# Attention in the second block: the values become the stationary operand, the turned probabilities move

## The reference

```python
def step(args):                       # causal, for 128 queries
    logits = jnp.einsum('bhqd,bhkd->bhqk', qc, k)
    if log_decay is not None:         # the forgetting attention
        logits = logits + args[2][..., None] - log_decay[:, :, None, :]
    logits = jnp.where(key_idx[None, :] <= q_idx[:, None], logits, -jnp.inf)
    p = jax.nn.softmax(logits, axis=-1)
    return jnp.einsum('bhqk,bhkd->bhqd', p, v)
# memory heads
p = jax.nn.softmax(jnp.einsum('bshd,bmhd->bhsm', q, k), axis=-1)
o_mem = jnp.einsum('bhsm,bmhd->bshd', p, v_mem)
x = x + jnp.concatenate([o_mix, o_mem], axis=-1) @ w_out[i]
```

## Time and profile before

| | us |
|---|---|
| median of 3 runs | 1580.07 |
| lowest and highest | 1578.89, 1580.39 |
| the profiled execution, its span from the first to the last instruction | 1580.1 |
| PE busy / DVE busy / ACT busy / POOL busy in it | 1545.3 / 824.7 / 736.3 / 322.4 |
| forgetting attention, about | 490 to 576 of the span |
| latent attention, memory heads, about | 1036 to 1077 of the span |
| latent attention, its 12 heads, about | 1077 to 1161 of the span |

### The profile page before, as it was taken

How to read it: one execution, slowest core, us unless ns; L and a number is a source line. 1 busy time by engine, 2 the same in 40 slices (tenths; PEclk the granted TensorE clock), 3 DMA queues, 4 the chain that set the end, 5 groups by cost and what they waited for, 6 DMA issues and landing times. The chain is left out here.

```text
span 1580.1 us, 22237 instructions
## 1 busy us (share of the span) xinstructions
PE 1545.3 (98%) x9054; PEld 1299.5 (82%) x9054; DVE 824.7 (52%) x1406; ACT 736.3 (47%) x1423; POOL 322.4 (20%) x273
## 2 busy tenths in 40 slices
PE   7999998999999999999999999999999999999999
PEld 6788787998898887788888888768887888888887
DVE  5355456556435755745334543668955644244442
ACT  4355445455654545544124443567845534133431
POOL 0000142001430001244013431032001343014420
PEclk9999999999999999999999999999999999999999
DMA  6202112323220103233223332110013333223331
GB/s 232 80 35 88 54 54 88 129 68 107 80 88 30 33 1 104 81 110 118 85 82 102 99 110 72 51 44 14 15 54 93 94 94 123 90 80 94 110 116 41
DMA packets 37462, 128.07 MB, mean 81 GB/s; under 512 B 4192, under 2 KB 8944, under 8 KB 37360
## 3 DMA queue, kind: packets, MB, share of 16 engines
q1 hardware_dynamic: 37360, 126.65, 25.3%
HBM read 124.54 MB, written 2.10 MB: 80 GB/s over the span
## 5 line engine op out<-in xcount | busy, mean ns | idle before, releaser
L321 PE MATMUL bank<-hhi,whi 128*128 128x512 f32 (+2 forms) x1064 | 419.4, 394 | 4.8 <-ACT hhi L1915 3.0
L323 PE MATMUL bank<-hhi,wlo 128*128 128x512 f32 (+2 forms) x1064 | 415.0, 390 | 0.0
L322 PE MATMUL bank<-hlo,whi 128*128 128x512 f32 (+2 forms) x1064 | 414.9, 390 | 0.0
L312 DVE TENSOR_TENSOR wlo<-wstage,whi 128x1024 fp32r<-128x1024 f32 (+9 forms) x250 | 278.6, 1117 | 129.4 <-ACT whi L302 129.0
L302 ACT CAST whi<-wstage 128x1024 fp32r<-128x1024 f32 (+9 forms) x250 | 236.1, 949 | 135.9 <-PE bank L323 131.2
L321 PEld LDWEIGHTS bank<-hhi,whi 128*128 128x128 f32 (+2 forms) x1064 | 199.2, 187 | 53.0 <-ACT hhi L1915 6.3
L2414 DVE SCALAR_TENSOR_TENSOR cr<-bank,vc,cr 128x511 f32<-128x511 f32 (+1 forms) x168 | 125.9, 749 | 217.1 <-ACT cr L2353 214.1
L323 PEld LDWEIGHTS bank<-hhi,wlo 128*128 128x128 f32 (+2 forms) x1064 | 199.0, 187 | 43.6
L322 PEld LDWEIGHTS bank<-hlo,whi 128*128 128x128 f32 (+2 forms) x1064 | 199.1, 187 | 41.4 <-issue 0.5
L2353 ACT ACTIVATE cr<-bank,vc 128x512 f32<-128x512 f32 x84 | 65.5, 780 | 248.5 <-PE bank L323 248.5
L2459 POOL TENSOR_TENSOR cr<-cr,cr 128x512 f32<-128x512 f32 x44 | 94.4, 2146 | 314.5 <-DVE cr L2414 279.8
(11 more groups left out here) (423 smaller groups left out, 2343.5 us busy)
## 6 DMA issues: line engine op xcount, KB each, us to landing
wstage<-in_wts SPq DMA_DIRECT2D x147, 512.0 KB, 3.6
wstage<-in_wts SPq DMA_DIRECT2D x32, 704.0 KB, 4.1
wstage<-in_wts SPq DMA_DIRECT2D x14, 768.0 KB, 4.3
xT<-in_x SPq DMA_DIRECT2D x4, 512.0 KB, 5.0
xt<-in_x SPq DMA_DIRECT2D x4, 512.0 KB, 6.6
out<-ob SPq DMA_DIRECT2D x8, 256.0 KB, 2.3
U<-in_rel_ext SPq DMA_DIRECT2D x6, 256.0 KB, 9.0
wstage<-in_wts SPq DMA_DIRECT2D x2, 603.0 KB, 3.8
```

The source lines that it names most:

```text
L312: e.tensor_tensor(K.wlo[i % 3][:, p], K.stage[i % 3][:, p], K.whi[i % 3][:, p].bitcast(F32), SUB).then_inc(*K.dve.up(("wlo", i) if last el ...
L321: e.matmul(o, lh, rh, start=start, stop=False)
L322: e.matmul(o, lh, rl, start=False, stop=False)
L323: return e.matmul(o, ll, rh, start=False, stop=stop)
```

## The change

The first attention ("att", in the first block) keeps its functions. The other two get a class of their own, `TurnedAttention`, and `pe_turned`, `act_turned`, `dve_turned` and `pool_turned`.

- The values are now the stationary operand (128 keys x 64 columns), and the turned probabilities of 256 queries move (items i = 0 and 1, or 2 and 3, lie side by side in one buffer). The two heads of a pair write to the partitions 0 to 63 and 64 to 127 of one bank, that is, they use the two column halves of the array. So `pv` runs once for a half of a pair (4 items), five steps after the half's last item, instead of once for each item.
- The outcome has features on the partitions at once. The transposes of y are gone. In exchange the factors (1 / row sum) must lie along the free side: GpSimd spreads the reciprocals over 64 columns each (128x512), TensorE turns that by four transposes, ScalarE copies it out, and VectorE multiplies the bank of the outcome by it in one product of 128x512.
- ScalarE makes hhi from SBUF, and hlo moves from VectorE to GpSimd.
- The reciprocal no longer waits for `pv` but for the exponentials.

```diff
-    def pv(t):
-        h, i = A.items[t]
...
-        for j in range(n // P):
-            for r in A.heads[h].v_ready(j):
+    def factors(p):
+
+        b = A.T.take(q, (A.name, "R", p))
+        q.wait_ge(*K.at((A.name, "spread", p)))
+        for i in range(4):
+            z = e.transpose(b[:, i * P:(i + 1) * P], A.y[A.name, "y", p][:, i * P:(i + 1) * P], K.ident[:])
+        z.then_inc(*K.pe.up((A.name, "R", p)))
+
+    def pv(p, g):
...
+        short, long = A.blocks(2 * p, 2 * g), A.blocks(2 * p, 2 * g + 1)
+        z = {}
+        for j in range(long):
...
+            c = 0 if j < short else P
+            for s in range(2):
+                o = K.bank((A.name, "O", p))[64 * s:64 * s + 64, (2 * g) * P + c:(2 * g + 2) * P]
+                z[s] = e.matmul(o, A.heads[2 * p + s].v(j), A.turned((p, g))[s][:, j, c:2 * P], start=j == 0, stop=j == long - 1)
...
-        if 5 <= t <= N + 4:
-            pv(t - 5)
-        p = A.post(t)
-        if p is not None:
-            q.wait_ge(*K.at((A.name, "fin", p)))
-            b = A.T.take(q, (A.name, "yT", p))
-            for c in range(4):
-                z = e.transpose(b[:, c * P:(c + 1) * P], A.y[A.name, "y", p][:, c, :], K.ident[:])
+        if A.done(t - 4) is not None:
+            factors(A.done(t - 4))
+        if t - 5 in A.ends:
+            pv(*A.ends[t - 5])
...
+        p = A.done(t - 5)
+        if p is not None:
+            act_evac(e, q, K, (A.name, "factors", p), (A.name, "R", p), A.y[A.name, "y", p][:], K.bank((A.name, "R", p))[:])
+        p = A.done(t - 7)
         if p is not None:
             kt = (p + 6) % 8
-            act_hi(e, q, K, (A.gen, "hi", kt), (A.name, "yT", p), K.hhi[:, kt, :])
+            q.wait_ge(*K.at((A.name, "fin", p)))
+            e.copy(K.hhi[:, kt, :], A.y[A.name, "y", p][:]).then_inc(*K.act.up((A.gen, "hi", kt)))
...
+        p = A.done(t - 2)
+        if p is not None:
+            rr = A.rs[:, 2 * p:2 * p + 2, :]
+            for item, (h, i) in enumerate(A.items):
+                if h // 2 == p:
+                    q.wait_ge(*K.at((A.name, "P", item)))
+            e.reciprocal(rr, rr).then_inc(*K.dve.up((A.name, "rr", p)))
+        p = A.done(t - 6)
+        if p is not None:
+            y = A.y[A.name, "y", p]
...
+            e.tensor_tensor(y[:], K.bank((A.name, "O", p))[:], y[:], MUL).then_inc(
+                *K.dve.up((A.name, "fin", p), frees=[(A.name, "O", p)]))
+def pool_turned(e, q, K, A):
+    for t in A.steps:
+        p = A.done(t - 3)
+        if p is not None:
+            y = A.y.take(q, (A.name, "y", p))
+            q.wait_ge(*K.at((A.name, "rr", p)))
+            e.tensor_copy(y[:].rearrange("p (i h n) -> p i h n", i=4, h=2),
+                          A.rs[:, 2 * p:2 * p + 2, :].rearrange("p h i -> p i h").unsqueeze(3).to_broadcast([P, 4, 2, 64])).then_inc(
+                *K.pool.up((A.name, "spread", p)))
+        p = A.done(t - 7)
+        if p is not None:
+            kt = (p + 6) % 8
+            q.wait_ge(*K.at((A.gen, "hi", kt)))
+            e.tensor_tensor(K.hlo[:, kt, :], A.y[A.name, "y", p][:], K.hhi[:, kt, :].bitcast(F32), SUB).then_inc(
+                *K.pool.up((A.gen, "lo", kt), frees=[(A.name, "y", p)]))
```

More of the change, by code:

```diff
@@ L1010, in __init__, with in_order @@
         self.last = [max(t for t, item in enumerate(self.items) if item[0] // 2 == p) for p in range(len(heads) // 2)]
-        self.given, self.pta = given, pta
         self.steps = range(-2, len(self.items) + 8)
+    def in_order(self):
+        out = []
+        for h in range(0, len(self.heads), 2):
+            order = [(i, s) for i in range(4) for s in range(2)] if self.heads[h].paired else [(i, s) for s in range(2) for i in range(4)]
+            out += [(h + s, i) for i, s in order]
+        return out
     def n(self, t):
@@ new lines, in act_att, with soft @@
+def act_att(e, q, K, A):
+    N = len(A.items)
+    def soft(t):
+        h, i = A.items[t]
+        n = A.n(t)
+        p = A.P.take(q, (A.name, "P", t))
+        q.wait_ge(*K.at((A.name, "mx", t)))
+        e.activation(p[:, 0:n], A.st[A.name, "s", t][:, 0:n], ACT.Exp, bias=A.mx[:, h, i:i + 1],
+                     accum_out=A.rs[:, h, i:i + 1]).then_inc(*K.act.up((A.name, "P", t), frees=[(A.name, "s", t)]))
+    for t in A.steps:
+        if 1 <= t <= N:
+            soft(t - 1)
+        if 3 <= t <= N + 2:
+            n = A.n(t - 3)
+            o = A.pt.take(q, (A.name, "pt", t - 3))
+            act_evac(e, q, K, (A.name, "pt", t - 3), (A.name, "T", t - 3), o[:, 0:n], K.bank((A.name, "T", t - 3))[:, 0:n])
+        yield
@@ L1148, in act_att @@
         if 3 <= t <= N + 2 and A.turned_on_act(t - 3):
[L1149 to L1151 removed]
+            act_evac(e, q, K, (A.name, "pt", t - 3), (A.name, "T", t - 3), *turned_to(A, q, K, t - 3))
         if A.prep(t):
@@ L1186, in finish @@
-    def finish(p, tiles):
-        b = K.bank((A.name, "O", p))
-        rr = A.rs[:, 2 * p:2 * p + 2, :]
-        if tiles[0] == 0:
-            q.wait_ge(*K.at((A.name, "pv", A.last[p])))
-            e.reciprocal(rr, rr).then_inc(*K.dve.up((A.name, "rr", p)))
-            if A.y is not None:
-                A.y.take(q, (A.name, "y", p))
-            q.wait_ge(*K.at((A.name, "rr", p)))
-        for i in tiles:
-            ov = b[:, :].rearrange("p (h i n) -> p h i n", h=2, i=4)[:, :, i, :]
-            e.tensor_tensor(A.out(p, i), ov, rr[:, :, i:i + 1].to_broadcast([P, 2, 64]), MUL).then_inc(
-                *K.dve.up((A.name, "fin", p) if i == 3 else (A.name, "fin", p, i), frees=[(A.name, "O", p)] * (i == 3)))
@@ L1201, in dve_att @@
-    late = 0 if A.st is not None else 1
-    for t in A.steps:
-        if late <= t < N + late:
-            soft(t - late)
-        p = A.post(t - 1)
-        if p is not None:
-            kt = (p + 6) % 8
-            dve_lo(e, q, K, (A.gen, "lo", kt), (A.name, "yT", p), (A.gen, "hi", kt), K.hlo[:, kt, :], K.hhi[:, kt, :])
+        q.wait_ge(*K.at((A.name, "S", t)))
+        e.tensor_reduce(m, K.bank((A.name, "S", t))[:, 0:n], AX, MAX, negate=True).then_inc(
+            *K.dve.up((A.name, "mx0" if A.heads[h].factor else "mx", t)))
```

230 lines of the change are left out of this document (157 added, 73 removed).

## The result

The changed kernel takes 1592.75 us at the median of 4 runs (1587.8 to 1594.53), beside 1580.23 for the kernel before on the same chip: ratio 1.0076, 95% interval 1.0055 to 1.0096. It is slower by 0.8%, where 1565.5 was forecast, and lies outside the range. The profiled execution took 1593.65 us, span 1591.9.

What follows compares the result with a forecast made beforehand. TensorE, working in 98% of the span, was taken to bound the kernel. Fox 5.2, latent causal heads 6.0 and memory heads 4.3, minus 1.0 at the end, made 14.5 us won: 1565.5 us, range 1554 to 1577.

Steps and rivals of the forecast that it cites:

- Removed and added products: TensorE, each attention: value products costing 33.7 us replaced by turned products costing 20.8, saving 12.9 us (8.1 to 17.7).
- the changes: TensorE, each attention: 32 switches between whole array and halves at 0.10 us, 3.2 us lost (bounds 0 and 3.2).
- column halves taking turns: Rival, turned products: the two heads stream one after the other, 0.86 us a block; 7.7 us slower, 1587.8; chance 0.11.
- loads in the open: Rival, turned products: weight loads cost the full 0.22 us a block; 6.5 us won, 1573.6; chance 0.15.
- the rival with the loads hidden: Rival, turned products: loads hidden and changes between array shapes free; 26.7 us won, 1553.5; chance 0.13.
- Mla's causal heads: Latent attention's 12 heads: PE gives back 7.7 us and still leads, with ACT within 4%; 6.0 us won.
- The added wait: TensorE's turning of factors waits for POOL's spread: fox loses 3.5 us (0 to 8); no wait in mla.
- Fox: Forgetting attention: 12.9 saved, less 3.2 for changes, 3.5 for waits and 1.0 at the end; 5.2 us won.
- Memory heads of the latent attention: 2.1 us from PE, 2.0 from a bank wait, 1.7 from the clock, less 1.5 for POOL's queue: 4.3 us won.
- Tails: End of each attention: nothing covers the wait for the factors there, 1 us more each.
- Hand-offs bind: Rival: spread 1 us late or more at every pair, or gaps lower the clock; 4 to 5 us left, 1576; chance 0.08.

Runs made afterwards that it cites:

- Experiment 4: Most value products left out: latent causal heads, kernel before, ratio 0.9988; same, changed kernel with factors in their own bank, 0.9986; fox causal heads, kernel before, 0.9941.
- kernel with the factors' bank: The changed kernel, with factors of the latent attention's causal pairs turned into a PSUM bank of their own: 1582.42 us, ratio 1.0023 to the kernel before.
- experiment 1: The change in one attention only, the other as in the kernel before: fox alone 1576.4 us, ratio 0.9977; latent alone 1590.13 us, ratio 1.0073.

## Why the prediction was wrong, point by point

- *Removed and added products* ("2.76 us a pair", "an attention saves 12.9", less 3.2 for the changes): right in mechanism, and conservative. The products give back 16.6 us in fox. Against that stand 3.4 us of changes behind turnings of probabilities and 0.7 behind those of factors (8 times 0.09), so 12.5 are left, where 9.7 was forecast. A change costs about what the earlier trace rows said.
- *Rivals on the price*: column halves taking turns (0.73 us a block or more) and loads in the open (0.65) are both out, at 0.40 a block; on this term the rival with the loads hidden was right. (The first of them is also priced unevenly: 0.215 us for 256 columns, where the 0.92 ns a column read from the same row makes 0.235. Nothing hangs on it.) By the page's rule (the Trainium skill, TensorE: Matmul & The Clock Gate, The mechanism) the four loads of a block, which share all rows, should have stood in line; the trace does not show that cost.
- *Mla's causal heads* ("PE still leads but ACT is within 4%, so I take 6.0"): the step that failed, with the next one. The latent stage was to win 9.3 us (6.0 + 4.3 - 1.0) and lost 11.6. The step compares sums of busy time and takes the largest for the bound, then moves the end of the stage by PE's relief. Experiment 4 shows that even 16 us off PE move it by 3.2. No engine's sum was the bound. What stood a few us behind PE's 80.7 of 84 was, by the waits, a chain over two score banks and two banks of turned probabilities; no run takes that chain apart link by link.
- *The added wait* (spread on POOL, "In mla ... no wait"): I priced what the factors' turning waits *for* and not what its result *holds*. POOL's spread, 0.61 us as forecast, made PE wait 0.7 us in all fox, once. The factors take one of two banks, and what frees it is ScalarE's copy, late in an ordered queue: 7.6 us of the latent stage (at most 3.4 of them the clock's). It was listed under "ACT gets one copy, 0.5 us more a pair", a cost of work where the cost was of place. The forecast named neither the bank nor who waits for it.
- *Fox* (5.2 forecast, 2.1 measured): PE gives 2.8 more than forecast (12.5 against 9.7), and the waits take some 11 us where 3.5 stood; that term is what failed here. Before, each step had value products to lay between one turning and the next; a pair's eight steps now have two bursts. That this is the reason is likely from experiment 4 (10.7 won in place, 2.1 gathered), but no run isolates it.
- *Memory heads of the latent attention* ("Together 4.3"): about 0.7 us by marks near 1080 us. The wait of 1.97 and the half clock of the earlier trace rows are gone as forecast (clock 1.00 in the second stretch above), but PE waits 2.0 us for ScalarE's copies of the values there and at 1077.8 us another 0.95 for the copy of the factors. Whether this stretch was bound by PE's work at all was not tested.
- *Tails* (1.0 each): right. In fox PE's projection starts 3.7 us after the last exponential's end in place of 3.0; in the latent attention 3.8 in place of 2.5 (kernel with the factors' bank).
- *Hand-offs bind* was the nearest rival, and it still came out faster, at 1576: it took 4 us off a gain in the latent stage that was not there. (Its sum is also off: 14.5 less 4.5 in fox and 4 in mla leaves 6.0, not 4 to 5, so 1574.) Its chance, 0.08, and the whole 0.12 for slower were too low for a change that adds a stage to a two-bank ring.

The clock has a share. Two stretches of the kernel after, with PE's gaps before the fall, and the last two bursts:

```profile
1160.00:1164.00 4.00, 3.04 (x22) 2.40 (x22) 3.25 (x8) 2.94 (x9) 0.00 (x0) 1.00 0.00 0
1164.00:1168.00 4.00, 2.93 (x15) 1.75 (x15) 2.28 (x7) 2.53 (x8) 1.88 (x2) 0.66 0.19 47
1168.00:1172.00 4.00, 4.00 (x20) 2.31 (x21) 0.61 (x1) 0.58 (x1) 0.00 (x0) 0.50 0.21 84
```

```profile
1167.81 1.55 PE L1258 MATMUL bank<-mla_pt,vt 128*64 128x256 f32 x8
1169.29 1.12 PE L1237 MATMUL bank<-ident,y 128*128 128x128 f32 x4
1170.34 2.57 PE L1258 MATMUL bank<-mla_pt,vt 128*64 128x256 f32 x16
1172.84 0.50 PE L321 MATMUL bank<-hhi,whi 128*128 128x512 f32 x1
```

At the level of 1.2 GHz the two bursts take 1.48 and 2.50 us from start to next start, 0.61 and 0.83 more than at 2.4. The profile after has 10.2 us of the latent stage at that level and the one before 6.8, so this is at most 2 us of the 11.6. Whether waits bring the clock down, as the order of the rows suggests, was not tested.

**What stays open**: how much of the remaining 4 us of latent loss (factors' bank kept apart) is the third score bank, and how much the unevenness of the steps. That the gathered products are on the path there is shown by leaving them out; why, with PE busy 73 of 84 us, is not. Splitting one burst did not help, but it still left steps without value products, as in experiment 1.

## What to carry to other kernels

A share of 96 or 98% says that an engine has work to put into its waits, not that the end moves when you take that work away. Before you cash in a saving, ask what the work covered: leave it out and time the kernel (one run here would have told 3 of 16 us in one stage and 11 of 16 in the other). That number is for work that goes and leaves the rest in its place. Where the change also gathers the rest into fewer, longer groups, it can win far less: 2 us in the stage that had 11 to give. And when a step writes into a ring of two banks, price the bank by the instruction that frees it and its place in its engine's queue, not by the write.

## What was not expected

- The length of a drawn record hides waits: in fox the same 152 turnings take 14.3 us more from start to next start. Changes to products in halves make 3.4 of them, and of the other 11 about 8 appear as idle time in the waits.
- Loads of 64 columns (132 to 137 ns each, against 190 to 192 in the earlier trace rows) cost nothing that can be seen: a burst of 16 products of mostly 256 columns takes 1.67 us.

```profile
L1258 PEld LDWEIGHTS bank<-fox_pt,fv x144: 132/137/137, 501.4 to 576.6; 128*64 128x64 f32 x144
```

- POOL's spread took 609 to 610 ns and its low part 1276 to 1286, as the earlier trace rows said for others of the shape.

```profile
L1381 POOL TENSOR_TENSOR hlo<-y,hhi 128x512 fp32r<-128x512 f32 x8 | 10.3, 1286 | 36.9 <-ACT hhi L1324 36.9
L1374 POOL COPY y<-fox_rs 128x512 f32<-128x512 f32 x8 | 4.9, 610 | 58.1 <-DVE fox_rs L1356 58.1
```
